# Two-layer hybrid encoder trunk: six query/key high places, and the first attention steps issued in another order

## The reference

```
xn  = rmsnorm(h, norm_mix[l])
u   = xn @ w_in[l]
branches = (attention_branch(...), conformer_branch(...), ssd_branch(...), fourier_branch(...))
for i, br in enumerate(branches):
    mixed = mixed + jax.nn.sigmoid(xn @ w_gate[l, i] + b_gate[l, i]) * br
h = h + mixed @ w_out[l]
xn = rmsnorm(h, norm_ffn[l])
h = h + (swiglu(xn, ...) if l % 2 == 0 else moe_swiglu(xn, ...))
h = h + sigmoid(h @ ple_gate[l]) * (p[l] @ ple_proj[l])
```

## Time and profile before

| | |
|---|---|
| median of 3 runs | 2198.56 us (2194.96 to 2199.19) |
| profiled execution, its own time | 2203.03 us |
| its span, first to last instruction | 2200.9 us |
| mean granted TensorE clock | 0.983 |
| PE, PEld, DVE, ACT busy | 97%, 87%, 75%, 59% |
| DMA | 533.15 MB, mean 242 GB/s |

### The profile page before, as it was taken

How to read it: one execution, slowest core, us unless ns; L and a number is a source line. 1 busy time by engine, 2 the same in 40 slices (tenths; PEclk the granted TensorE clock), 3 DMA queues, 4 the chain that set the end, 5 groups by cost and what they waited for, 6 DMA issues and landing times.

```text
span 2200.9 us, 36743 instructions
## 1 busy us (share of the span) xinstructions
PE 2133.7 (97%) x13368; PEld 1912.0 (87%) x13368; DVE 1656.4 (75%) x2356; ACT 1304.1 (59%) x1820; POOL 24.0 (1%) x44
## 2 busy tenths in 40 slices
PE   6999999989998999999999999999999999999997
PEld 6999899989998999899888888888888888888886
DVE  3997555655446997555568898888889888888885
ACT  4545544454435545444457777777777777777773
POOL 0000000000000000100000000000000000000000
PEclk9999999999999999999989999999999999999998
DMA  6533434455445434335449899898999989898982
GB/s 243 171 132 137 142 130 191 153 194 189 152 154 177 173 116 149 114 145 205 160 187 349 330 347 369 328 365 332 346 340 354 356 336 352 344 356 330 344 320 77
DMA packets 74963, 533.15 MB, mean 242 GB/s; under 512 B 8655, under 2 KB 8655, under 8 KB 11000
## 3 DMA queue, kind: packets, MB, share of 16 engines
q1 hardware_dynamic: 72620, 525.04, 63.3%
q0 software_dynamic: 2048, 6.29, 1.5%
q10 hardware_dynamic: 204, 0.54, 0.1%
HBM read 530.74 MB, written 1.10 MB: 242 GB/s over the span
## 4 chain that ended last, share of the span: by engine, by line
PE 88%; DVE 9%; ACT 2%; DMA 1%; issue 0%; DVEq 0%; SPq 0%; ACTq 0%
PE ps L844 25%; PE ps L846 25%; PE ps L845 25%; PE ps L532 7%; DVE cvfa L1684 3%; PE ps L1011 1%; PE ps L1040 1%; DVE ring_lo L1795 1%; PE ps L792 1%; DVE ring_lo L1636 1%; PE ps L538 1%; PE ps L805 1%; DVE xn L1628 1%; ACT ex L1307 0%; DVE rstd L1622 0%
## 5 line engine op out<-in xcount | busy, mean ns | idle before, releaser
L2004 DVE TENSOR_TENSOR wlo<-ring,whi 128x1024 fp32r<-128x1024 f32 x746 | 873.0, 1221 | 144.0 <-ACT whi L1450 143.5
L1450 ACT ACTIVATE whi<-ring 128x1024 fp32r<-128x1024 f32 x746 | 749.5, 1055 | 141.4 <-PE ps L846 130.7
L844 PE MATMUL ps<-whi,xhi 128*128 128x512 f32 (+1 forms) x1160 | 439.3, 379 | 0.5 <-DVE xlo L2130 0.5
L846 PE MATMUL ps<-whi,xlo 128*128 128x512 f32 (+1 forms) x1160 | 429.4, 370 | 0.0
L845 PE MATMUL ps<-wlo,xhi 128*128 128x512 f32 x904 | 356.9, 395 | 0.0
L844 PE MATMUL ps<-xhi,whi 128*128 128x256 f32 x1024 | 294.7, 288 | 19.3 <-DVE xlo L1650 12.8
L845 PE MATMUL ps<-xlo,whi 128*128 128x256 f32 x1024 | 290.6, 284 | 0.0
L846 PE MATMUL ps<-xhi,ring_lo 128*128 128x256 f32 x928 | 264.7, 285 | 0.0
L846 PEld LDWEIGHTS ps<-whi,xlo 128*128 128x128 f32 x1160 | 219.0, 189 | 40.4
L844 PEld LDWEIGHTS ps<-whi,xhi 128*128 128x128 f32 x1160 | 219.4, 189 | 35.2 <-DVE xlo L2130 0.9
L844 PEld LDWEIGHTS ps<-xhi,whi 128*128 128x128 f32 x1024 | 197.7, 193 | 21.8 <-issue 12.0
(11 more groups left out here) (263 smaller groups left out, 3594.9 us busy)
## 6 DMA issues: line engine op xcount, KB each, us to landing
ring<-w_experts SPq DMA_DIRECT2D x340, 1024.0 KB, 5.9
ring<-w_mixers SPq DMA_DIRECT2D x114, 1024.0 KB, 5.0
ring<-w_dense SPq DMA_DIRECT2D x33, 1024.0 KB, 4.8
ring<-w_ple SPq DMA_DIRECT2D x10, 1024.0 KB, 4.8
bias<-bias_rows POOLq DMA_DIRECT2D x8, 256.0 KB, 6.6
cvfa<-bias_rows POOLq DMA_DIRECT2D x8, 256.0 KB, 5.0
constants_sb<-constants SPq DMA_DIRECT2D x1, 1048.0 KB, 7.7
h<-x_in SPq DMA_DIRECT2D x1, 1024.0 KB, 5.3
```

Of the source, the lines that this page charges most:

```text
L844: pe.matmul(dst, lhs[0], rhs[0], start=first, stop=False, skip_group_check=True)
L846: return pe.matmul(dst, lhs[1], rhs[0], start=False, stop=last, skip_group_check=True)
L1450: act.activation(whi[:, slot, :], ring[:, j % RING, lo:lo + UNIT], ACT.Copy).then_inc(s_wh, 1)
L2004: dve.tensor_tensor(wlo[:, slot, :], ring[:, j % RING, lo:lo + UNIT], whi[:, slot, :], ALU.subtract).then_inc(s_wl, 1)
```

## The change

Six places for the query/key highs: `query_key_high` keeps four, two more (`query_key_high_x`) lie at the address of `xn`. A block's high is now written after PE has used block j - 3; the high of block 19 comes before the first round, with a wait for tile `T_DT` alone. Each round makes five lows: 1, 1, 1, 2. In `ssm_out` DVE makes the lows of gate block 0 ahead of the reciprocal; dual 0's `biased` stands ahead of the lows of gate block 1, and ACT's `probs` of dual 0 ahead of the highs of gate block 1. PE's wait for `ybr` (`s_ybs`) moves from the head of `attention` to dual 0's transposes; at the head it waits for the copies of all projection tiles instead.

```
-QK_SLOTS = 4
+QK_SLOTS = 6
+QK_AHEAD = QK_SLOTS // 2
...
+        with nc.sbuf_tensor("query_key_high_x", [P, 2, UNIT], F32R) as qhx:
+            pass
         xn = sb("xn", [P, KT, SEQ])
...
-            return qhi[:, (2 * (j - EARLY_BLOCKS) + u) % QK_SLOTS, :]
+            slot = (2 * (j - EARLY_BLOCKS) + u) % QK_SLOTS
+            return qhx[:, slot - 4, :] if slot >= 4 else qhi[:, slot, :]
...
@@ PE transposes @@
                     if d:
                         pe.wait_ge(s_tc, n - 1)
+                    else:
+                        pe.wait_ge(s_ybs, l + 1)
@@ PE attention @@
-                pe.wait_ge(s_ybs, l + 1)
+                pe.wait_ge(s_pf, l * N_PROJ + N_PROJ)
@@ ACT query_key_highs @@
-                if j >= EARLY_BLOCKS + 2:
-                    act.wait_ge(s_pj, l * N_PROJ + (T_Q + 2 * (j - EARLY_BLOCKS) - 2))
+                if j >= EARLY_BLOCKS + QK_AHEAD:
+                    act.wait_ge(s_pj, l * N_PROJ + (T_Q + 2 * (j - EARLY_BLOCKS - QK_AHEAD) + 2))
+                elif j == EARLY_BLOCKS + QK_AHEAD - 1:
+                    act.wait_ge(s_pj, l * N_PROJ + T_DT + 1)
@@ ACT query_key @@
-                    query_key_highs(l, EARLY_BLOCKS + t // 2 + 2)
+                    query_key_highs(l, EARLY_BLOCKS + t // 2 + QK_AHEAD)
@@ ACT query_key_heads @@
+                query_key_highs(l, EARLY_BLOCKS + QK_AHEAD - 1)
                 for hh in range(SSM_HEADS // SSM_GROUPS):
...
                 m.then_inc(s_ybs, 1)
+                probs(l, 0)
                 gate_highs(l, 1)
@@ ACT attention @@
-                probs(l, 0)
                 for d in range(DUALS):
@@ DVE ssm_heads @@
-                    head_mix(l, hh, n, 0)
-                    query_key_lows(l, 1)
-                    head_mix(l, hh, n, 1)
-                    query_key_lows(l, 1)
+                    for g in range(SSM_GROUPS):
+                        head_mix(l, hh, n, g)
+                        query_key_lows(l, 1)
...
-                    query_key_lows(l, 3 if hh % 2 else 1)
+                    query_key_lows(l, 2)
@@ DVE ssm_out @@
+                gate_lows(l, 0)
                 dve.wait_ge(s_ya, l + 1)
                 dve.reciprocal(yst[:, 6:8], yst[:, 4:6]).then_inc(s_yc, 1)
...
-                gate_lows(l, 0)
+                for u in range(2):
+                    biased(l, 0, u)
                 gate_lows(l, 1)
@@ DVE attention @@
-                for u in range(2):
-                    biased(l, 0, u)
                 for d in range(DUALS):
```

More of the change, by code:

```diff
@@ L165, in trunk_program @@
         cst = sb("constants_sb", [P, CK])
-        with nc.sbuf_tensor("query_key_high", [P, QK_SLOTS, UNIT], F32R) as qhi:
+        with nc.sbuf_tensor("query_key_high", [P, 4, UNIT], F32R) as qhi:
             pass
```

## The result

The changed kernel takes **2181.49 us**, the median of 4 runs (2179.92 to 2181.66); the kernel before, run beside it, 2198.27 (2194.96 to 2199.19). The ratio is 0.9925, with a 95% interval of 0.9908 to 0.9942: 16.8 us less. A second set of runs gave 2181.87 against 2199.29, again 0.9925 (0.9911 to 0.9938). The forecast was 2178.7 (2174.5 to 2185.5): the direction and the range hold, the value is 2.8 us too low. The changed kernel's profiled execution took 2181.59 us, 21.4 less than the profiled one of before (2203.03).

The account below looks back on a forecast made before the run. PE, busy 97% of the span, was taken as the bound, so gains lay only in its waits and half-speed clock. 6.9 + 3.4 + 7.9 + 1.7 = 19.9 us off the median 2198.6 gave 2178.7 us, range 2174.5 to 2185.5.

Parts of the forecast that it names:

- Idle time at the lows: Query/key tiles: PE's three waits for lows go in each layer, 3.5 + 3.4 = 6.9 us.
- unit 10: Query/key round 1: this low moves to the first slot, ending at 173.8, at least 0.6 us before PE wants it.
- the late unit: Rival, query/key round 1: unit 10 still late, tile 8 stops again and the clock with it; 2186.5 at worst, chance 0.07.
- the first high not freed: Rival, query/key: block 19's high must wait, rounds 0 and 1 stay, only attention's start gains; 2187.5, chance 0.02.
- Clock at tile 8: Half-speed stretches around 180 and 832 us, behind the 2.08 us wait, go: 1.7 + 1.7 = 3.4 us.
- Start of attention: First transpose of y to dual 0's next scores falls from 10.56 to 6.61 us: 2 x 3.95 = 7.9 us.
- a dear table load: Rival, attention's start: a drain ends ACT's exponentials 1.38 us later, PE waits about 0.95 a layer; 2180.6, chance 0.10.
- Clock at layer 1's attention: Layer 1's half-speed stretch at 899 us, attention's start, goes: 1.7 us, bounds 0 and 1.7.
- I take the same 19.9 from the median: Whole kernel: the profiled execution's summed gain is also subtracted from the median, 2198.6 - 19.9 = 2178.7 us.
- the clock does not pay back: Rival: waits go but half-speed stretches come elsewhere, 1.7 to 5.1 off the gain; 2180.4 to 2183.8, chance 0.16.
- The slower rival: Rival, attention's start: gate block 0's lows ahead of y's reciprocal make y late and PE stop; 2204, chance 0.01.
- What would show it: Signs in the changed profile: no low waits, full query/key clock, about 6.6 us at attention's start, shifts of 9 to 11 and about 20.

Follow-up runs that it names:

- att_pe_only: Kernel before with only PE's wait for ybr moved to dual 0's transposes, ACT's and DVE's order unchanged: 2203.52 us, ratio 1.0022.
- att_order_only: Kernel before with only ACT's and DVE's order at attention's start changed, PE's wait for ybr left at the head: 2194.69 us, ratio 0.9985.
- pe_only_again: Second run of the kernel before with only PE's wait for ybr moved: 2203.16 us, ratio 1.0022.
- six_old_lows: Changed kernel with attention's part undone and the old counts of lows a round, six places kept: 2193.35 us, ratio 0.9971.
- six_old_lows_full: Changed kernel, attention's part included, with the old counts of lows a round and six places: 2186.46 us, ratio 0.9948.
- att_only: Kernel before with only attention's part of the change made, query/key highs and lows as before: 2190.3 us, ratio 0.9957.
- qk_only: Changed kernel with attention's part undone, so only the query/key part of the change: 2189.68 us, ratio 0.996.
- four_two_lows: Kernel before, four places kept, with two lows in round 1's first slot and none in its second: 2195.07 us, ratio 0.9986.

## Why the prediction was right, and where its number was off

*Idle time at the lows, 6.9 us: right.* All three waits went in both layers. In traces where the stretch at half speed is missing, Q falls from 128.14 to 124.55, so the idle time was 3.6 a layer, against 3.5 and 3.4 in the sum. Round 0's low came without a wait, unit 10 moved as described. The rivals of the late unit and of the first high not freed fall.

*Clock at tile 8, 3.4 us: right for the kernel before, a little too large.* Q0 and Q1 are 1.55 us longer where the stretch is there, so 3.1 us and not 3.4. In the kernel before it was there in six places of six; over all traces with tile 8's wait of 2.1 us in 10 of 14 (missing in one of two places of `att_pe_only` and of `att_order_only`, and in both of `pe_only_again`); never in the ten places without a wait there, nor in the four of `six_old_lows` and `six_old_lows_full`, where it was 1.2 to 1.3 us.

*Start of attention, 7.9 us: right.* A0 fell by 3.8 to 4.0 from any trace of before to any of the changed kernel, A1 by 3.9 where neither had half speed. The exponentials were through 4.7 and 5.4 us after the first transpose of y, where the sum had about 4.8 and 5.7. The rival of a dear table load falls: `att_only` and the changed kernel show no wait, and the exponential starts 0.01 us behind the 1.28 us load. The 1.38 us of drain that the Trainium skill (ScalarE: Activation LUTs, What ACT_TABLE_LOAD costs) adds did not stand between the load and the exponential here, nor ahead of the load, which starts 0.02 us after the copies' end (233.09 + 1.57 = 234.66).

*Clock at layer 1's attention, 1.7 us: the mis-sized term.* It was in the first profiled execution of before alone, one of three. The step that failed is the one that read "I take the same 19.9 from the median". For the profiled execution it was a good sum: 19.9 predicted, 19.7 found in the four stretches, and 21.4 in the executions' own times with 1.8 from the rest. The median does not carry the term: the other two executions give 5.2 + 3.9 + 5.1 + 3.9 = 18.1, and 16.8 to 17.4 were measured. That leaves 0.7 to 1.3 us by which the rest of the changed kernel must be the longer one in the medians; since the rest differs by up to 5.7 us between executions of one kernel, the traces can't say where. The granted clocks on record help one step further. Runs with a recorded clock of 0.987 take 2196.3 us on average before the change (18 runs) and 2181.3 after it (5 runs), those with 0.986 take 2198.1 (14 runs) and 2181.9 (4 runs): 15.0 and 16.2 less at an equal clock, beside the 2 x (3.6 + 3.9) = 15.0 of idle time that the stretches show. So the idle time was gained in full, and of the 5.1 us of the two clock terms only about 1 to 2 reached the median (an estimate; the recorded clocks are rounded to 0.001). That some of the 3.1 us gained at tile 8 is lost again elsewhere fits this, but no trace shows the place. The text had this case among its rivals, *the clock does not pay back* (1.7 to 5.1 less, 2180.4 to 2183.8), at a chance of 0.16, and its sentence on the Trainium skill (TensorE: Matmul & The Clock Gate, Part 1: The HAM clock gate) said it outright: one stretch more or less in the median. The traces agree: 1 of 6 places at the start of attention in before's three traces.

*The slower rival: no price at all.* Gate block 0's lows ahead of the reciprocal had 2.4 us to spare and cost nothing.

*What would show it: all of it was there.* No wait for lows, clock 1.00 over the query/key tiles, 6.47 us for a forecast of 6.6, gate block 1's lows behind both `biased` with PE busy; the shift is 441.75 - 431.89 = 9.9 us at the end of layer 0's attention and 1095.01 - 1073.88 = 21.1 at that of layer 1, for 9 to 11 and about 20.

## What to carry to other kernels

Cut the spans of two traces at instructions that stand at fixed places of the program, and compare stretch by stretch: a change then shows to 0.1 us what the total hides under several us. Expect in a median only what more than one execution shows; a stretch at half speed that one trace has and the next lacks belongs in the range, not in the sum. And move a wait only together with the work that it waited for: PE's wait alone lost 4 to 5 us, the steps of ACT and DVE alone gained 3.9, and the two together 8.6.

## What was not expected of the hardware

The length of PE's stops alone does not say whether the granted clock falls to half, 1.2 GHz, behind them. At tile 8 it fell behind a stop of 2.1 us in 10 of 14 places, and behind one of 1.2 to 1.3 us in none of 4. At attention's start, behind stops of 1.7, 0.9 and 0.9 us, it fell in 1 of 6 places of before, but in 4 of 6 of `qk_only`, `six_old_lows` and `four_two_lows`, where it had stayed full at tile 8. Behind one stop of 2.8 us and a shorter one it fell in 4 of 4, in three of them for 6.7 or 6.8 us (0.28 x 12 x 2 and 0.34 x 10 x 2 of the windows above) where the shorter stops never brought more than 3.4; but in three of these four too the clock had stayed full at tile 8. Counted by tile 8, in all 16 of these places, the clock fell at attention's start in 2 of the 7 places that had half speed there, and in 7 of the 9 that had not. Whether the longer stop, the missing stretch before it, or both bring it about, no run here separates. Removing all of the waits, in ten places of the kernels that have attention's part whole, left none.
